# Preparing the cached attention inside the last prompt head of a hybrid decoder step

## The reference

```python
def mla_prompt_attention(q_nope, q_rope, lat, k_rope, w_uk, w_uv):      # 8 heads, 8 tiles of 128 queries
    k_nope = jnp.einsum('btc,chd->bthd', lat, w_uk)
    v = jnp.einsum('btc,chd->bthd', lat, w_uv)
    ...
    s = (q_nope @ k_nope + q_rope @ k_rope) * SOFTMAX_SCALE, causal
    p = softmax(s);  o = p @ v

def mla_sample_attention(q_nope, q_rope, lat, k_rope, w_uk, w_uv, lat_past, kr_past):
    q_lat = jnp.einsum('bshd,chd->bshc', q_nope, w_uk)                   # the turned key weights act on q
    s_past = (jnp.einsum('bshc,btc->bhst', q_lat, lat_past)
              + jnp.einsum('bshr,btr->bhst', q_rope, kr_past)) * SOFTMAX_SCALE
    ...
    o_lat = p[..., :T] @ lat_past + p[..., T:] @ lat
    o = jnp.einsum('bshc,chd->bshd', o_lat, w_uv)

lat_past = cache_latent[l][page_table]     # 8 sequences x 32 pages of 128 keys, 256 numbers a key
kr_past = cache_krope[l][page_table]       # 32 numbers a key
```

## Time and profile before

| | us |
|---|---|
| median of 3 runs | 1626.76 |
| lowest, highest | 1626.31, 1629.55 |
| the profiled execution's own time | 1635.51 |
| its span, first to last instruction | 1633.7 |
| mean granted TensorE clock | 0.957 |

### The profile page before, as it was taken

How to read it: one execution, slowest core, us unless ns; L and a number is a source line. 1 busy time by engine, 2 the same in 40 slices (tenths; PEclk the granted TensorE clock), 3 DMA queues, 4 the chain that set the end, 5 groups by cost and what they waited for, 6 DMA issues and landing times.

```text
span 1633.7 us, 23652 instructions
## 1 busy us (share of the span) xinstructions
PE 1508.7 (92%) x9745; PEld 1349.9 (83%) x9745; DVE 693.6 (42%) x1460; ACT 426.9 (26%) x901; POOL 399.2 (24%) x300
## 2 busy tenths in 40 slices
PE   4359977899989999998999999999999999999998
PEld 3149966666657666766999999999999999999997
DVE  2772175656544343434666323323232332323245
ACT  2232143555543333332314011020201102020134
POOL 0420240222233111106023332050504215050400
PEclk9579988899997999998999999999999999999999
DMA  8510112322326344534201211030301103020102
GB/s 308 216 61 1 54 49 77 113 96 92 114 100 241 117 164 147 167 132 125 76 26 39 65 44 60 1 104 1 91 14 52 53 2 103 1 91 14 39 1 110
DMA packets 90441, 137.16 MB, mean 84 GB/s; under 512 B 13755, under 2 KB 64903, under 8 KB 86103
## 3 DMA queue, kind: packets, MB, share of 16 engines
q1 hardware_dynamic: 79343, 85.07, 16.1%
q0 software_dynamic: 7872, 46.14, 7.9%
q10 hardware_dynamic: 3120, 4.46, 0.8%
HBM read 121.98 MB, written 13.79 MB: 83 GB/s over the span
## 4 chain that ended last, share of the span: by engine, by line
PE 85%; DVE 7%; DMA 3%; issue 2%; ACT 2%; SPq 0%; DVEq 0%; ACTq 0%
PE psa L1244 23%; PE psa L1258 23%; PE psa L1222 6%; PE psa L1094 4%; PE psa L1121 4%; PE psa L1161 3%; PE psa L844 3%; PE psa L827 3%; PE psa L1003 2%; PE psa L967 2%; PE psa L1124 2%; DMA wmod<-in_w_mod 2%; DVE sqb L413 1%; PE psa L988 1%; PE psa L433 1%
## 5 line engine op out<-in xcount | busy, mean ns | idle before, releaser
L1244 PE MATMUL psa<-hhi,wr 128*128 128x384 f32 (+1 forms) x1536 | 374.7, 327 | 0.0
L1244 PEld LDWEIGHTS psa<-hhi,wr 128*128 128x128 f32 x1536 | 270.9, 188 | 0.1
L1258 PE MATMUL psa<-g_hi,wd_hi 128*128 128x384 f32 (+1 forms) x768 | 251.5, 328 | 0.0
L1244 PE MATMUL psa<-hlo,wr 128*128 128x384 f32 (+1 forms) x768 | 250.6, 326 | 0.0
L1258 PE MATMUL psa<-g_hi,wd_lo 128*128 128x384 f32 (+1 forms) x768 | 250.5, 326 | 0.0
L1258 PE MATMUL psa<-g_lo,wd_hi 128*128 128x384 f32 (+1 forms) x768 | 250.5, 326 | 0.0
L2062 DVE SCALAR_TENSOR_TENSOR xT<-psa,modT,xT 128x384 f32<-128x384 f32 (+1 forms) x216 | 123.2, 571 | 191.3 <-PE psa L1258 160.9
L1641 ACT ACTIVATE g_relu<-psa 128x384 f32<-128x384 f32 (+1 forms) x96 | 45.4, 473 | 600.9 <-PE psa L1244 600.9
L615 POOL TENSOR_SCALAR wr<-wraw 128x1024 fp32r<-128x1024 f32 x34 | 36.4, 1070 | 571.2 <-PE psa L1244 492.9
L2127 DVE TENSOR_TENSOR psa<-psa,g_relu 128x384 f32<-128x384 f32 (+1 forms) x96 | 52.2, 544 | 261.6 <-ACT g_relu L1641 261.6
L1244 PEld LDWEIGHTS psa<-hlo,wr 128*128 128x128 f32 x768 | 144.2, 188 | 0.1
(11 more groups left out here) (331 smaller groups left out, 2521.9 us busy)
## 6 DMA issues: line engine op xcount, KB each, us to landing
wmod<-in_w_mod SPq DMA_DIRECT2D x8, 2048.0 KB, 7.9
wraw<-in_w_up SPq DMA_DIRECT2D x32, 512.0 KB, 4.0
wraw<-in_w_down SPq DMA_DIRECT2D x32, 512.0 KB, 3.2
wmod<-in_w_mod POOLq DMA_DIRECT2D x4, 2048.0 KB, 14.8
x_scr<-xT SPq DMA_DIRECT2D x1, 4352.0 KB, 21.3
xstage<-in_x_prompt SPq DMA_DIRECT2D x8, 512.0 KB, 8.6
wraw<-in_w_out SPq DMA_DIRECT2D x8, 512.0 KB, 4.1
out_y_p<-yst SPq DMA_DIRECT2D x8, 512.0 KB, 2.7
```

Source lines behind the costliest of these rows:

```text
L1244: mm = pe.matmul(out[:, :N], w[:, c * P:c * P + P], x[:, c, c0:c0 + N], start=(c == 0 and q == 0), stop=(c == KD - 1 and q == 2))
L1258: mm = pe.matmul(out[:, :N], w[:, c, n * P:n * P + P], x[:, c, c0:c0 + N], start=(c == 0 and q == 0), stop=(c == FG - 1 and q == 2))
```

## The change

- SP loads `qs` and `wuk_all` at the end of the prompt attention's loads, without a meeting ahead; they go to places in the x buffer (X0) that are free by then.
- TensorE turns half of the key weights ahead of `turn(63)`, the other half, the queries and the mask behind it, into banks 4 to 7, and only then runs `mods_back(7)` and `values(7, 1)`. The products for `q_lat` follow. One meeting (3) is left, where meeting 4 was.
- ScalarE's copies to `wukT` stand ahead of `out_lo(7, 1)`; VectorE's copy of the queries, the clearing and filling of `qr4` and the mask stand ahead of the last modulation and `out_sum(7, 1)`. `latn` is summed at the start of the prompt attention.
- GpSimd comes to the meeting right behind the last `prob`, but does not wait there: it requests the first two groups of pages of sequence 0 (the latents beneath are no longer used, `k_mm`), then both rotary pages (when all scores are made, `s_mm`), then, when the values are no longer used (`pv_mm`), the other two groups, and only then waits for the meeting and requests sequence 1.
- Sequence 0 now uses the lower half of `page`; `pkr0` and `latn` move into the h buffer (H0); the places of `wo_low` and `wo_mid` are swapped accordingly.

```diff
-    qs = at("qs", [TS, H * DQ], F32, R0 + 73728)
-    wuk_all = at("wuk_all", [P, CC, H * DN], F32, R0 + 76800)
+    qs = at("qs", [TS, H * DQ], F32, X0 + 17920)
+    wuk_all = at("wuk_all", [P, CC, H * DN], F32, X0 + 20992)
...
-    pkr = (at("pkr0", [P, PAGES, DR], F32, R0 + 65536), at("pkr1", [P, PAGES, DR], F32, H0 + 18432))
+    pkr = (at("pkr0", [P, PAGES, DR], F32, H0 + 24576), at("pkr1", [P, PAGES, DR], F32, H0 + 18432))
...
             mods_in(hh)
-        barrier(sp, 3)
         sp.dma_start(qs[:, :], q_scr[PT, 0:TS, :]).then_inc(sem("s4_in"), 16)
         sp.dma_start(wuk_all[:, :, :], w_uk.rearrange("(k p) n -> p k n", p=P)).then_inc(sem("s4_in"), 16)
-        barrier(sp, 4)
+        barrier(sp, 3)
...
             u = b % 2
-            g.indirect_dma_start(page[:, 1 - u, 8 * j:8 * j + 8, :].rearrange("p r c -> p (r c)"), None, lat_rows,
+            g.indirect_dma_start(page[:, u, 8 * j:8 * j + 8, :].rearrange("p r c -> p (r c)"), None, lat_rows,
...
+        arrive(g)
+        g.wait_ge(sem("k_mm"), H)
+        g.wait_ge(sem("latn"), 1)
+        for j in range(2):
+            gather(0, j)
+        g.wait_ge(sem("s_mm"), NT)
         gather_rope(0)
-        for j in range(4):
+        gather_rope(1)
+        g.wait_ge(sem("pv_mm"), 2 * H)
+        for j in range(2, 4):
             gather(0, j)
-        gather_rope(1)
-        barrier(g, 4)
+        g.wait_ge(sem("stage_done"), 5 * 3)
...
+        def turn_wuk(k):
+            for u in range(2):
+                h = 2 * k + u
+                for c in range(CC):
+                    mm = pe.transpose(bank(4 + k)[0:DN, u * C + c * P:u * C + c * P + P],
+                                      wuk_all[:, c, h * DN:h * DN + DN], ident[:, :])
+            mm.then_inc(sem("wukT_mm"), 1)
...
+            if i == NT - 1:
+                pe.wait_ge(sem("s4_in"), 32)
+                pe.wait_ge(sem("exp"), NT - 1)
+                turn_wuk(0)
+                turn_wuk(1)
             turn(i)
-        mods_back(H - 1)
-        values(H - 1, 1, range(8))
-        barrier(pe, 3)
...
+        turn_wuk(2)
+        turn_wuk(3)
+        pe.wait_ge(sem("wukT_ev"), 1)
         for h in range(H):
             mm = pe.transpose(bank(4)[0:DQ, h * TS:h * TS + TS], qs[:, h * DQ:h * DQ + DQ], ident[0:TS, 0:TS])
         mm.then_inc(sem("qsT_mm"), 1)
+        pe.wait_ge(sem("wukT_ev"), 4)
         pe.transpose(bank(7)[0:64, 0:NS], mask_new[:, :], ident[0:NS, 0:NS]).then_inc(sem("mask_mm"), 1)
+        mods_back(H - 1)
+        values(H - 1, 1, range(8))
         pe.wait_ge(sem("wukT_ev"), 4)
         pe.wait_ge(sem("qsT_ev"), 1)
...
-        barrier(pe, 4)
+        barrier(pe, 3)
...
-        out_lo(H - 1, 1)
-        barrier(act, 3)
...
+        out_lo(H - 1, 1)
         act.wait_ge(sem("qsT_ev"), 1)
         act.wait_ge(sem("qr_clear"), 1)
...
         rope_lo(0)
+        tt(latn[:, :, :], latT_hi[:, :, TP:T].bitcast(F32), latT_lo[:, :, TP:T].bitcast(F32), ALU.add).then_inc(sem("latn"), 1)
```

More of the change, by code:

```diff
@@ L291, in build @@
     oT = at("oT", [P, CC, H, NB, NS], F32, X0 + 28736)
-    latn = at("latn", [P, CC, TS], F32, X0 + 32832)
+    latn = at("latn", [P, CC, TS], F32, H0 + 32768)
     o_b = at("o_b", [P, C], F32, X0 + 33344)
@@ L303, in build @@
     page = at("page", [P, 2, PAGES, C], F32, R0)
-    pkr = (at("pkr0", [P, PAGES, DR], F32, R0 + 65536), at("pkr1", [P, PAGES, DR], F32, H0 + 18432))
+    pkr = (at("pkr0", [P, PAGES, DR], F32, H0 + 24576), at("pkr1", [P, PAGES, DR], F32, H0 + 18432))
     lat_new = at("lat_new", [NS, 2, C], F32, R0 + 69632)
     wuv_all = at("wuv_all", [P, CC, H * DV], F32, R0 + 65536)
-    wo_low = at("wo_low", [P, 2, 2, KD * P], F32R, R0)
-    wo_mid = at("wo_mid", [P, 4, 2, KD * P], F32R, R0 + 32768)
+    wo_low = at("wo_low", [P, 2, 2, KD * P], F32R, R0 + 32768)
+    wo_mid = at("wo_mid", [P, 4, 2, KD * P], F32R, R0)
     wr = at("wr", [P, 3, 2, KD * P], F32R, R0 + 67584)
@@ L689, in _ @@
                 split_wuk(hh // 2 + 1)
-        barrier(g, 3)
         lat_rows = cache_lat.rearrange("n (q r) c -> (n q) (r c)", r=8)
@@ L1052, in _ @@
                 scores(i + 2)
-            turn(i)
-        mods_back(H - 1)
-        values(H - 1, 1, range(8))
-        barrier(pe, 3)
-        pe.wait_ge(sem("s4_in"), 32)
-        for h in range(H):
-            for c in range(CC):
-                mm = pe.transpose(bank(h // 2)[0:DN, (h % 2) * C + c * P:(h % 2) * C + c * P + P],
-                                  wuk_all[:, c, h * DN:h * DN + DN], ident[:, :])
-            if h % 2:
-                mm.then_inc(sem("wukT_mm"), 1)
+            if i == NT - 1:
[3 more added lines that the diff above has]
+                turn_wuk(1)
+            turn(i)
+        turn_wuk(2)
+        turn_wuk(3)
+        pe.wait_ge(sem("wukT_ev"), 1)
         for h in range(H):
@@ L1094, in keys @@
                     mm = pe.transpose(bank(G % 3)[:, j * P:j * P + P],
-                                      page[:, 1 - b % 2, 8 * k + 4 * (i // 2) + j, i % 2 * P:i % 2 * P + P], ident[:, :])
+                                      page[:, b % 2, 8 * k + 4 * (i // 2) + j, i % 2 * P:i % 2 * P + P], ident[:, :])
                 mm.then_inc(sem("t_mm"), 1)
@@ L1160, in times_latents @@
                 for h in range(2):
-                    mm = pe.matmul(bank(6)[64 * h:64 * h + 64, 0:C], pT[:, j % 2, t, h, :], page[:, 1 - b % 2, 8 * j + 4 * h + t, :],
+                    mm = pe.matmul(bank(6)[64 * h:64 * h + 64, 0:C], pT[:, j % 2, t, h, :], page[:, b % 2, 8 * j + 4 * h + t, :],
                                    start=(j == 0 and t == 0), stop=(h == 1 and j == NPAIR - 1 and t == TILES - 1))
@@ L1520, in _ @@
                 exponentials(i + 2)
-        out_lo(H - 1, 1)
-        barrier(act, 3)
         for k in range(4):
             act.wait_ge(sem("wukT_mm"), k + 1)
-            act.activation(wukT[:, 2 * k:2 * k + 2, :], bank(k)[0:DN, :].rearrange("p (h c) -> p h c", h=2), ACT.Copy)\
+            act.activation(wukT[:, 2 * k:2 * k + 2, :], bank(4 + k)[0:DN, :].rearrange("p (h c) -> p h c", h=2), ACT.Copy)\
                .then_inc(sem("wukT_ev"), 1)
+        out_lo(H - 1, 1)
         act.wait_ge(sem("qsT_ev"), 1)
@@ L1536, in _ @@
                        bank(5).rearrange("p (h b s) -> p b h s", h=H, b=NB), ACT.Copy)
-        barrier(act, 4)
+        barrier(act, 3)
         def keys_turned(n, h):
@@ L1934, in _ @@
         the_rest(NT - 1)
-        mods_in(H - 1)
-        out_sum(H - 1, 1)
-        barrier(v, 3)
         v.wait_ge(sem("qsT_mm"), 1)
@@ L1942, in _ @@
         v.memset(qr4[:, :, :, :], 0.0).then_inc(sem("qr_clear"), 1)
-        tt(latn[:, :, :], latT_hi[:, :, TP:T].bitcast(F32), latT_lo[:, :, TP:T].bitcast(F32), ALU.add)
-        tt(ident2[:, :], ident[:, 0:64], ident[:, 64:128], ALU.add)
         v.wait_ge(sem("mask_mm"), 1)
@@ L1951, in _ @@
                           qsT[DN:DQ, :].rearrange("p (h b s) -> p b h s", h=H, b=NB))
+        mods_in(H - 1)
+        out_sum(H - 1, 1)
+        tt(ident2[:, :], ident[:, 0:64], ident[:, 64:128], ALU.add)
         v.wait_ge(sem("ql_mm"), 2)
@@ L1954, in _ @@
                       bank(6).rearrange("p (h b s) -> p b h s", h=H, b=NB))
-        barrier(v, 4)
+        barrier(v, 3)
         def keys_turned(n):
```

## The result

| | before | changed |
|---|---|---|
| median, us | 1629.55 | 1619.04 |
| lowest, highest | 1626.31, 1634.03 | 1614.69, 1622.61 |
| runs | 9 | 9 |
| the profiled execution's own time | 1635.51 | 1619.33 |
| its mean granted clock | 0.957 | 0.964 |

The ratio is 0.9938, with a 95% interval of 0.9924 to 0.9952: 10.1 us less (7.8 to 12.4). Three later comparisons gave 0.9918, 0.9933 and 0.9925, so 10 to 13 us, in the mean of the four 11.7. The prediction said 1613.8; the measured time is 5.2 above it and just outside the upper end of the range, 1619.0.

What follows compares the result with a forecast made beforehand. The prediction took serial preparation before the first keys, partly idle and at half clock, as the bound: 33.1 us becoming 17.2, so 15.9 less, minus 2.9 for the clock, is 13.0; 1626.76 - 13.0 = 1613.8 us, range 1609.5 to 1619.0.

Steps and rivals of the forecast that it cites:

- the new wait: Behind `turn(63)`, TensorE waits for ScalarE's fourth copy of turned weights, ahead of mask, `mods_back` and values; costs 1.1 us.
- Steps 1 to 3: On TensorE: eight weight transposes (0.9 us), `turn(63)` and remaining turning to 481.3, then mask, `mods_back(7)` and values to 485.4.
- Step 4: The 32 recorded products behind the values: 3.54 us at full clock, half of 7.07, bounds 3.1 to 4.0; to 489.0.
- Step 5: Copy and meeting behind the products: 0.8 us, the same as before, GpSimd and SP having arrived long before; to 489.8.
- D: Distance from the end of the last modulation piece to the first scores; forecast to fall from 33.1 us to 20.1.
- Step 6: Turning the first two pairs of keys behind the meeting: 4.24 us at full clock, 2.12 a pair; to 494.0.
- The pages: Early page requests land almost in time for the keys: at worst 0.7 us exposed, groups 2 and 3 up to 1.5.
- Rival C: Early page requests are served only when the values end, landing at 497.6: about 8 us less, 1619; chance 0.08.
- The clock: Low clock around the meeting nearly always, a second dip on the values in four of ten; takes back 2.9 us.
- rival A: The clock holds between modulation and first scores, no dip: the whole 15.9 us is saved, 1610.9; chance 0.17.
- rival B: Transposes do not hold the clock, so modulation, values, products and first keys run at half: 4.1 us saved, 1622.7; chance 0.05.

Runs made afterwards that it cites:

- e15: The changed kernel unchanged, run once more for a profile against the kernel before; ratio 0.9925.
- e4: The kernel before with only the loads of `qs` and `wuk_all` moved to the x buffer and ahead of meeting 3; ratio 1.0000.
- e5: The changed kernel, but GpSimd arrives at the one meeting behind its six requests instead of ahead; ratio to before 0.9967.
- e2: The changed kernel unchanged, run once more for a profile against the kernel before; ratio 0.9918.
- e3: The changed kernel with all page requests of sequence 0 issued behind the one meeting; ratio to before 0.9999.
- e10: The changed kernel, but VectorE arrives ahead of its copy of `q_f` and first scores wait on a semaphore of their own; ratio to before 0.9943.
- e1: The kernel before, unchanged, run once more for a profile against itself; ratio 0.9986.
- e13: The kernel before with 7 unread filler products on TensorE in front of its wait for the key weights; ratio 1.0009.
- e6: The kernel before with the two loads moved ahead of meeting 3 and GpSimd arriving at meeting 4 ahead of its requests; ratio 0.9956.
- e9: The changed kernel unchanged, run a third time against the kernel before; ratio 0.9933.
- e7: The changed kernel with the 16 products placed two by two between the eight tiles of `values(7, 1)`; ratio to before 1.0021.

## Why the prediction was right or wrong

**The steps.** Distances from the end of the modulation piece, in us:

| | forecast, full clock | e15 (no dip) | changed (dip) |
|---|---|---|---|
| `turn(63)` starts | 0.9 | 1.0 | 1.0 |
| mask, behind the new wait | 4.5 | 4.0 | 4.0 |
| values end | 8.6 | 8.4 | 8.4 |
| products end | 12.2 | 12.1 | 12.6 |
| keys start | 13.0 | 12.9 | 13.4 |
| first scores | 17.2 | 17.0 | 19.8 |

- *Steps 1 to 3 were right*, each within 0.5 us; the new wait for ScalarE was there, 0.72 in TensorE's row in place of 1.1.
- *Step 4, the products:* 3.75 at full clock (e4), 3.73 in the chain of e15, where I took half of 7.07, 3.54, in bounds of 3.1 to 4.0. Right.
- *Step 5, the meeting:* 0.8, right in size. Its side remark, that GpSimd "arrived long before", holds for the changed kernel because `arrive(g)` was put ahead of the requests. e5 shows that this line is worth 4.1 us of D. I had counted its cost at nothing without naming what would stand there without it.
- *Step 6, the keys:* 4.12 at full clock (e2), forecast 4.24. Right.
- *The pages:* no wait for a transfer in the changed kernel, as forecast. Rival C's sum was wrong: a wait of 7.8 taken off 13.0 leaves 5.2, and with half a dip more (0.85) 4.4, so 1622.4; I wrote 8 and 1619, which is 15.9 less 7.8 and leaves the clock out. e3, with late pages, leaves nothing. `pkr0` landed at 501.62 there, later than rival C's 497.6, since the requests there come behind the meeting (489.67), not behind the values. Two smaller slips changed nothing: page groups 2 and 3 are late by 0.7 at worst by the prediction's own figures (497.7 against 497), not 1.5, and its waits add up to 1.9, not 2.1.
- *The clock:* one dip around the meeting was expected nearly always, a second on the values in four of ten, 2.9 us in all. Four profiles have one dip (2.8 us) twice and none twice, so 1.4 in the mean: rival A, the clock holds, had 0.17 and should have had about half. The rule of the Trainium skill weighed in the prediction ("TensorE: Matmul & The Clock Gate", "Why this matters for your kernels"), that gaps this short do not lower the clock, isn't what decided: in the changed kernel the clock fell within the 32 products, ahead of the gap, with PE busy 1.92 of 2.00. The rule of the Trainium skill in the same page's Part 4, "PE-mode transpose", that transposes do not count as activity, is the one behind rival B's 1622.7; the profiles without a dip run through 25 transposes ahead of the values and 36 of keys at 1.00, against it.

The miss of 5.2 has two parts: the base was 2.8 too low, and the saving of 13.0 was 2.5 too large by the two medians of the comparison (1629.55 - 1619.04 = 10.5).

**What failed: the base.** The forecast took 13.0 off the median of three runs, 1626.76, and its first paragraph assumed that other executions pass the place as the profiled one did. The same kernel had medians of 1629.55, 1631.12, 1628.94 and 1630.16 in the four comparisons, 1629.9 in the mean. The base was 2.8 too low in the comparison that counted, which is more than half of the miss of 5.2; with 1629.55 the forecast would have read 1616.6. I took the range's lower end from the scatter of the three runs, but gave the upper end none. The upper end, 1619.0, was rival C's time with the wrong sum; with 1622.4 it would have held the measured 1619.04.

**What failed: the size of the saving, a little.** 13.0 was forecast; 10.1 was measured first, 11.7 in the mean of four (single ones 10.1 to 13.4). The start that I measured from was the longest of four: D is 33.0 in that profile and 32.0 to 32.4 in the three others, since the keys there waited for VectorE's copy, at 502.74, and in the others for GpSimd. That is 0.8 of it. The local difference of the four profiles each is 14.0, 2.3 more than the time shows. So the term that I added up, the distance, came out a little larger than forecast, and what failed is the step from it to the whole time. I can't settle this rest. GpSimd in VectorE's way, as in e10, accounts for about 0.6 us in one of the four, e15. Profiles of one program differ by as much elsewhere, in steps: from the first `turn` of the prompt attention to the last modulation piece it is 184.8 to 185.1 us in 12 of the 18 profiles and 186.6 to 186.7 in the other 6. It is one dip more, in the first head, as in that of before:

```profile
302.00:306.00 4.00, 3.36 (x13) 1.87 (x14) 2.11 (x5) 3.21 (x6) 1.27 (x2) 0.77 0.00 0
306.00:310.00 4.00, 4.00 (x19) 2.29 (x17) 3.48 (x4) 2.60 (x4) 0.65 (x1) 0.50 0.01 2
```

where e1 stands at 1.00 throughout. Four profiles of a side are too few to average such steps out.

**Near, for a partly wrong reason.** The prediction read the old 33 us as one serial path (transfer of the weights, slow clock, meeting) and took each piece of it as gain. Beside it ran GpSimd's path: meeting 3, six requests, the end of their transfers. Two of the pieces alone brought nothing, the loads (e4) and the clock (e13), and the same arithmetic would have forecast several microseconds for either. That the forecast came near is luck in this point: the change happened to cut both paths.

## What to carry to other kernels

Before a path in front of a meeting is priced, look at when every engine arrives, also those that the chain does not show: a releaser that is last by 0.7 us hides another. GpSimd, when it had requested its indirect transfers and then drained, arrived only when they were over (11.2 us behind the last request in e1), so let it arrive ahead of the requests, where the buffers allow it. And take the base of a forecast from as many runs as the verdict will have, or widen the range by their scatter on both sides.

## What the runs showed of the hardware

- GpSimd's drain behind indirect requests lasts until their transfers end: 11.2 us behind the last of six requests in e1, 8.6 in e4, 7.1 in e5, so it is no fixed time; the DMA share had fallen to 0.08 (e1, 496 to 498), 0.03 (e4, 498 to 500) and 0.31 (e5, 492 to 494) when it ended. Further requests don't wait for them (changed kernel: 490.95, 2.8 us behind the one before, as soon as the meeting was over).
- One of the page requests took 3.54 us in e4 (482.98) and 2.89 in e6 instead of 0.94, and both times VectorE cleared and filled `qr` then. By the Trainium skill ("SBUF — State Buffer", the section "SBUF: two separate sides") VectorE's faster copies between places of SBUF shut GpSimd out of a shared port while it writes the descriptors of its transfers. That alone doesn't cover it: in e4 the request would have been over at 483.92, while the first such copy (`qr` from `qsT`) starts at 485.93, behind the clearing (483.81, 1.76 us). Nor is it the clearing alone: in the changed kernel that ran (481.77, 1.76 us) beside a request at 482.09 that took 0.94. The cause is open.
- VectorE can be held by GpSimd: a copy of 64x4 numbers took 0.27 to 2.14 us in place of 0.17 in seven profiles in which it started while GpSimd split weights, and ended with GpSimd's instruction (e10: 514.96 and 514.94).
- 32 small products with PE wholly busy, or nearly, were no safe cover for the clock: it fell within them in the changed kernel, e9, e6 and e13 and held in e2, e4 and e15, with the same products; the changed kernel, e9, e2 and e15 are the same program.
- Value tiles that write the two halves of a bank's rows in turn take 3.15 us for eight; each of the 512-wide ones alone takes 1.0 (e7).
